# A chunked delta-rule recurrence: two tiles' triangular inverses by 128-wide levels, one tile after the other, or together from 64x64 blocks

## The reference, cut to what matters

```
mod = silu(c) @ ada_w + ada_b              # (1024) @ (1024 x 6144): six rows of 1024
h = rms_norm(x) * (1 + sc1) + sh1          # rows 0, 1: needed first
x = x + g1 * (concat[y_fox, y_rwkv] @ w_out)   # rows 2 to 5: needed after the recurrence
...
def step(S, inp):                          # per head, S is 64x64
    Sa = S @ a_t
    S = S * w_t + Sa (x) b_t + v_t (x) k_t
    return S, S @ r_t
```

## Time and profile before

| | |
|---|---|
| median of 3 runs | 1511.95 us |
| profiled execution, its own time | 1506.93 us |
| its span, first to last instruction | 1505.1 us |
| mean granted TensorE clock | 0.974 |
| PE busy | 1420.7 us, 94% of the span, 7774 MATMUL records |
| DVE busy | 686.7 us, 46% |
| ACT busy | 396.9 us, 26% |
| POOL busy | 121.8 us, 8% |

### The profile page before, as it was taken

The page is one execution under the profiler, slowest core; times in us unless marked ns, Lnnn a source line. Parts: engine busy times, 40 slices in busy tenths (PEclk is TensorE's granted clock), DMA queues, the critical chain, the costliest instruction groups (busy, mean ns, idle before and its releaser), DMA issues.

```text
span 1505.1 us, 19811 instructions
## 1 busy us (share of the span) xinstructions
PE 1420.7 (94%) x7774; PEld 948.3 (63%) x7774; DVE 686.7 (46%) x1234; ACT 396.9 (26%) x636; POOL 121.8 (8%) x67
## 2 busy tenths in 40 slices
PE   5999998899899999999999999999999998999997
PEld 2545698887455444444444444587778657699985
DVE  2054567455761222222222222475356834577763
ACT  0221433300002222222222222245231211354443
POOL 0013346600000000000000000300000000000000
PEclk9999999999989999999999999989979999999999
DMA  9682124411735999999999998555250322155552
GB/s 338 224 270 84 57 82 157 155 57 57 313 144 202 412 418 412 417 413 422 414 413 419 415 412 360 184 210 168 92 104 1 113 75 94 60 193 188 177 195 84
DMA packets 94258, 338.80 MB, mean 225 GB/s; under 512 B 9738, under 2 KB 34842, under 8 KB 65398
## 3 DMA queue, kind: packets, MB, share of 16 engines
q1 hardware_dynamic: 84178, 319.08, 55.1%
q10 hardware_dynamic: 7845, 12.03, 3.1%
q0 software_dynamic: 2176, 6.86, 1.3%
HBM read 332.94 MB, written 1.05 MB: 222 GB/s over the span
## 4 chain that ended last, share of the span: by engine, by line
PE 82%; DVE 12%; DMA 3%; issue 1%; ACT 1%; ACTq 0%; DVEq 0%
PE bank L1751 15%; PE bank L1325 10%; PE bank L1767 8%; PE bank L1340 6%; PE bank L1341 6%; PE bank L1342 6%; PE bank L1311 4%; PE bank L1714 3%; PE bank L1715 2%; PE bank L1732 2%; PE bank L1734 2%; DMA small<-in_norm_g 2%; PE bank L1563 2%; PE bank L1352 2%; PE bank L1567 1%
## 5 line engine op out<-in xcount | busy, mean ns | idle before, releaser
L1325 PE MATMUL bank<-ring,xT 128*128 128x512 f32 (+2 forms) x448 | 182.5, 562 | 8.1 <-DVE xT L2232 5.2
L1325 PEld LDWEIGHTS bank<-ring,xT 128*128 128x128 f32 x448 | 83.4, 195 | 96.0 <-issue 82.8
L1311 PE MATMUL bank<-c_ident 128*128 128x128 f32 (+1 forms) x986 | 132.6, 290 | 0.0
L1311 PEld LDWEIGHTS bank<-c_ident 128*128 128x128 f32 x986 | 126.7, 206 | 5.1 <-issue 4.2
L1767 PE MATMUL bank<-dn,tmp 128*64 128x512 f32 x528 | 120.6, 598 | 0.0
L2763 DVE TENSOR_TENSOR xT<-bank,mod 128x512 fp32r<-128x512 f32 x66 | 45.6, 691 | 158.0 <-ACT mod L1074 150.7
L2756 DVE SCALAR_TENSOR_TENSOR tmp<-silu_c,rc,bank 128x256 f32<-128x256 f32 x33 | 22.6, 684 | 196.8 <-ACT silu_c L1061 191.4
L1340 PE MATMUL bank<-mod,w_high 128*128 128x256 f32 x352 | 98.6, 280 | 1.7 <-DVE xT L3246 1.7
L1341 PE MATMUL bank<-xT,w_high 128*128 128x256 f32 x352 | 98.6, 280 | 0.0
L1342 PE MATMUL bank<-mod,ring 128*128 128x256 f32 x352 | 98.2, 279 | 0.0
L3233 DVE TENSOR_TENSOR ring<-ring,w_high 128x1024 fp32r<-128x1024 f32 x66 | 77.7, 1220 | 21.8 <-ACT w_high L1260 20.1
(11 more groups left out here) (634 smaller groups left out, 2536.0 us busy)
## 6 DMA issues: line engine op xcount, KB each, us to landing
dn<-in_exp_w_down SPq DMA_DIRECT2D x66, 1024.0 KB, 10.4
ring<-in_exp_w_gate SPq DMA_DIRECT2D x34, 1024.0 KB, 10.1
ring<-in_exp_w_up SPq DMA_DIRECT2D x34, 1024.0 KB, 12.1
gu_odd<-in_exp_w_gate SPq DMA_DIRECT2D x32, 1024.0 KB, 9.9
gu_odd<-in_exp_w_up SPq DMA_DIRECT2D x32, 1024.0 KB, 12.0
ring<-in_w_ffn_in SPq DMA_DIRECT2D x22, 1024.0 KB, 5.0
ring<-in_ada_w SPq DMA_DIRECT2D x16, 1024.0 KB, 4.9
ring<-in_w_in SPq DMA_DIRECT2D x7, 2048.0 KB, 11.9
```

The lines of the kernel that those rows point to most:

```text
L1311: pe.matmul(bank[b][:, lo:lo + width], cst["ident"][:, :], cst["ident"][:, 0:width], start=True, stop=True, skip_group_check=True)
L1325: mm = pe.matmul(bank[lin_bank(o)][:, 0:n], lhs(k, t), ring[:, j % RING, k * n:(k + 1) * n], start=(k == 0), stop=(k == kt - 1 and not bias))
```

## The change

Both tiles go through the inverse together. The folded arrays `invs[t]` and `amat[t]` hold, for 8 heads, the two 64x64 diagonal blocks of the 128x128 matrix on top of each other: rows 0 to 63 for the first, 64 to 127 for the second, 8 x 64 = 512 columns. Every product of levels 1 to 5 becomes two products of 64x64 operands (r = 0, 1), one in the upper left and one in the lower right quarter of the array, written to partitions 0 to 63 and 64 to 127 of one bank. All eight heads of a tile fit one bank, so a level has two groups: the two tiles. Level 6 is replaced by a merge: two 64x64 products per head, with a ScalarE copy after each, give the block below the diagonal (`last`), and the solve works with the parts. The products for gram 1 to 3 (`value_grams`) are issued between the levels' products; the first matrices are only made for the diagonal blocks.

The late units are done as `ada_unit` does them: four products of a 32-column weight tile per unit on TensorE, 16 units, ten of them among heads 4 to 7 in place of `keep_warm` products, six behind the heads. There are four slots. The ScalarE scaling, the GpSimd sums and GpSimd's `memset` go. The bias comes in by a load on ScalarE's queue and a VectorE add (`late_sums`). The eight row products stand behind the last read-out instead of in tile 1's levels. The gates of the fox heads move on VectorE from level 2 and 3 of tile 0 to behind the state.

```diff
+    folded += [lv[level][0:BS, 0:BS][np.arange(P) % BS] for level in range(LAST + 1)]
...
-        gram = sb("gram", [P, HEADS, 4, P], wkv_stack)
-        amat = sb("amat", [P, HEADS, P], wkv_stack)
-        inv = sb("inv", [P, HEADS, P], wkv_stack)
-        invT = tmp[:, :].rearrange("p (h c) -> p h c", h=HEADS)
+        gram = (sb("gram", [P, HEADS, 4, P], wkv_stack), gram_1)
+        invs = [sb(f"invs{t}", [P, 2, HEADS, BS], wkv_stack) for t in range(T)]
+        amat = [logw[:, t, :].rearrange("p (h c) -> p h c", c=BS) for t in range(T)]
+        last = [tmp[:, t * W1:(t + 1) * W1].rearrange("p (h c) -> p h c", c=BS) for t in range(T)]
...
+                if u < LATE_SLOTS:
+                    sp.wait_ge(lin_mm, last_of(J_VR if u < LATE_SLOTS // 2 else J_G))
+                else:
+                    sp.wait_ge(late_used, u - LATE_SLOTS + 1)
+                sp.dma_start(late_slot[u % LATE_SLOTS],
+                             A["ada_w"][k * P:(k + 1) * P, (batch + 1) * 2 * D:(batch + 2) * 2 * D])\
+                    .then_inc(ada_full[1 + u % LATE_SLOTS], 16)
...
-            stream(J_OUT, J_OUT + 1)
-            sp.wait_ge(lin_mm, after(("row", N_ROWS - 1)))
-            stream(J_OUT + 1, J_OUT + 2)
+            stream(J_OUT, J_OUT + 2)
...
+            for t in range(T):
+                act.wait_ge(wkv_mm, wkv_count(t, LAST + 1))
+                act.activation(amat[t][BS:P, :, :], heads8(bank[6 + t][BS:P, :]), ACT.Copy).then_inc(wkv_w, 1)
+            for t in range(T):
+                act.wait_ge(wkv_mm, wkv_count(t, LAST + 1, 1))
+                act.activation(last[t][0:BS, :, :], heads8(bank[4 + t][0:BS, :]), ACT.Copy).then_inc(wkv_upd, 1)
...
+            def late_units(n):
+
+                for u in range(late_n[0], late_n[0] + n):
+                    batch, k = u // KT, u % KT
+                    if k == 0:
+                        pe.wait_ge(cb_ready, 2)
+                        pe.wait_ge(lin_evac, after(J_G, batch))
+                    pe.wait_ge(ada_full[1 + u % LATE_SLOTS], 16 * (u // LATE_SLOTS + 2))
+                    for g in range(4):
+                        mm = pe.matmul(bank[batch][32 * g:32 * (g + 1), :], late_cols[:, k, :],
+                                       late_slot[u % LATE_SLOTS][:, g * BANK:(g + 1) * BANK],
+                                       start=(k == 0), stop=(k == KT - 1))
+                    mm.then_inc(late_used, 1)
+                late_n[0] += n
...
-                keep_warm((0, 0, 0, 0, 32, 14, 4, 4)[h], 2, W1 - HD, HD)
+                if h >= 4:
+                    late_units(2)
+                    keep_warm((12, 6, 0, 0)[h - 4], 2, W1 - HD, HD)
...
-                    keep_warm(16 if h == 6 else 0, 2, W1 - HD, HD)
+                    if h == 6:
+                        late_units(2)
...
+            def first_matrices(t):
+
+                banks = (score_bank(), score_bank())
+                for pair in range(4):
+                    for r in range(2):
+                        for g in range(2):
+                            src = tilT_of(t, pair)
+                            mm = pe.matmul(banks[g][halves[r], block_of(pair)], src[halves[g], AT_, halves[r]],
+                                           src[halves[g], BT_, halves[r]], start=True, stop=True)
...
+            def value_grams(n):
+
+                t, pair = n // 4, n % 4
+                pe.wait_ge(gram_evac, 2 * n)
+                src = tilT_of(t, pair)
+                for i, (w, v) in enumerate(((BT_, RT_), (KTT_, AT_), (KTT_, RT_))):
+                    for g in range(2):
+                        mm = pe.matmul(bank[g][:, i * P:(i + 1) * P], src[halves[g], w, :], src[halves[g], v, :],
...
+            def masked_source(t, level):
+
+                pe.wait_ge(wkv_upd, T * (level - 1) + t + 1)
                 for h in range(HEADS):
+                    for r in range(2):
+                        mm = pe.matmul(bank[6 + t][halves[r], block_of(h)], gram[t][halves[r], h, 0, halves[r]],
+                                       invs[t][halves[r], INV, h, :], start=True, stop=True)
...
+            def updates(t, level):
+
+                pe.wait_ge(wkv_w, T * level + t + 1)
+                for h in range(HEADS):
+                    for r in range(2):
+                        mm = pe.matmul(bank[4 + t][halves[r], block_of(h)], amat[t][halves[r], h, :],
+                                       invs[t][halves[r], INV_T, h, :], start=True, stop=True)
+                for h in range(HEADS):
+                    for r in range(2 if level < LAST else 1):
+                        mm = pe.matmul(bank[2 + t][halves[r], block_of(h)], invs[t][halves[r], INV_T, h, :],
+                                       amat[t][halves[r], h, :], start=True, stop=True)
+                mm.then_inc(wkv_mm, 1)
...
+            late_units(2)
+            til_transposes(0)
+            late_units(1)
+            pe.wait_ge(tp_evac, TP_TIL + 4)
+            first_matrices(0)
+            til_transposes(1)
+            transposed_grams(0)
+            pe.wait_ge(fox_out, 1)
+            first_transposes(0)
+            late_units(2)
+            pe.wait_ge(tp_evac, TP_TIL + 8)
+            first_matrices(1)
+            transposed_grams(1)
+            first_transposes(1)
+            late_units(1)
+            pe.wait_ge(sc_evac, SC_GRAM + 4 * T)
+            pe.wait_ge(late_summed, 2)
+            for level in range(1, LAST + 1):
+                for t in range(T):
+                    masked_source(t, level)
+                for t in range(T):
+                    if level < LAST:
+                        value_grams(T * (level - 1) + t)
+                    elif t == 0:
+                        pe.wait_ge(lerp_done, 4)
+                        pe.wait_ge(gram_evac, 2 * 4 * T)
+                        value_products(0, bank[0], 2, True).then_inc(u_mm, 1)
+                    updates(t, level)
+            value_products(1, bank[1], 2, False)
+            for t in range(T):
+                pe.wait_ge(wkv_upd, T * LAST + t + 1)
                 for h in range(HEADS):
+                    mm = pe.matmul(bank[6 + t][halves[1], block_of(h)], gram[t][halves[0], h, 0, halves[1]],
+                                   invs[t][halves[0], INV, h, :], start=True, stop=True)
+                mm.then_inc(wkv_mm, 1)
+            value_products(0, bank[2], 3, False)
+            for t in range(T):
+                pe.wait_ge(wkv_w, T * (LAST + 1) + t + 1)
                 for h in range(HEADS):
+                    mm = pe.matmul(bank[4 + t][halves[0], block_of(h)], amat[t][halves[1], h, :],
+                                   last[t][halves[1], h, :], start=True, stop=True)
+                mm.then_inc(wkv_mm, 1)
+            value_products(1, bank[3], 3, False)
+            pe.wait_ge(u_evac, 1)
+            solved(0, bank[7])
+            keep_warm(4, 4)
+            pe.wait_ge(u_evac, 2)
+            b = score_bank()
+            for pair in range(4):
+                c = slice(pair * P, (pair + 1) * P)
+                pe.matmul(b[:, c], til(BT_, 0)[:, c], rhs_u[:, 1, c], start=True, stop=False)
+                mm = pe.matmul(b[:, c], til(KTT_, 0)[:, c], z_rw[:, 0, 1024 + pair * P:1024 + (pair + 1) * P],
+                               start=False, stop=True)
+            mm.then_inc(sc_mm, 1)
+            read_out(0, bank[2])
+            pe.wait_ge(state_ready, 1)
+            with_state(bank[1], AT_).then_inc(u_mm, 1)
+            with_state(bank[3], RT_)
+            keep_warm(4, 4)
+            pe.wait_ge(u_evac, 4)
+            solved(1, bank[0])
+            keep_warm(4, 4)
+            pe.wait_ge(u_evac, 5)
+            read_out(1, bank[3])
+            for i in range(N_ROWS):
+                o, r = outputs[(("row", i), 0)], slice(i % 4 * 32, i % 4 * 32 + 1)
+                pe.wait_ge(lin_evac, o - 1)
+                pe.matmul(bank[lin_bank(o)][:, :], ones_pp[r, :], late_rows[i // 4][r, :], start=True, stop=True)\
+                    .then_inc(lin_mm, 1)
...
-                pool.tensor_tensor(sums, sums, late_slot[u % 2], ALU.add).then_inc(late_used, 1)
...
+            dve.wait_ge(lin_mm, last_of(J_G))
+            dve.tensor_copy(late_cols, small[:, KT:2 * KT].unsqueeze(2).broadcast_to([P, KT, 32])).then_inc(cb_ready, 1)
...
+                    dve.tensor_tensor(invs[t][:, INV_T, :, :], invs[t][:, INV_T, :, :], a, ALU.add)
+                    link(dve.tensor_tensor(invs[t][:, INV, :, :], invs[t][:, INV, :, :], b, ALU.add))
+                else:
+                    low, high = slice(0, BS), slice(BS, P)
+                    dve.tensor_tensor(invs[t][low, INV, :, :], invs[t][low, INV, :, :], b[low], ALU.add)
+                    dve.tensor_tensor(last[t][high, :, :], invs[t][high, INV_T, :, :], a[high], ALU.add)
+                    link(dve.tensor_tensor(invs[t][low, INV_T, :, :], invs[t][low, INV_T, :, :], a[low], ALU.add))
...
+            til_copies(0)
+            head_outputs()
```

(35 more changed lines are left out.)

354 lines of the change are left out of this document (145 added, 209 removed).

## The result

| | before | after |
|---|---|---|
| median of 5 runs | 1511.95 us | 1455.22 us (1452.51 to 1465.5) |
| profiled execution, its own time | 1506.93 us | 1465.5 us |
| its span | 1505.1 us | 1463.2 us |
| mean granted clock | 0.974 | 0.960 |
| PE busy | 1420.7 us | 1376.7 us, 8116 records |

The ratio is 0.9639 (95% interval 0.9607 to 0.967): faster, by 56.7 us between the medians. The profiled execution lay 10 us above its median, so I read stages from it and totals from medians.

The account below looks back on a forecast made before the run. TensorE was taken as the bound, its levels limited by chained products and masks. The changed part was to end at 307.0 instead of 368.5 us, saving 61.5: 1506.9 - 61.5 + 5.0 = 1451 us, range 1438 to 1486.

Parts of the forecast that it names:

- both tiles' inverses in one stretch, halves overlapping: Levels of both tiles: 64x64 row halves overlap, 0.0325 us per record; 61.5 us saved in all; chance 0.50.
- the slow rival: Levels 1 to 5: small products cost 0.11 us per record, 0.0785 more for 1056 records; 1538 us; chance 0.12.
- The 64x64 record: Small products of the levels: alternating halves cost 0.0325 us per record; ends 0.0275 and 0.055, for safety 0.11.
- starts of the two halves within 0.02 us: Sign that the forecast is right: in the levels, the two row halves' products start nearly together.
- The same-bank rival: Levels: halves writing one bank take turns, 0.0225 us more per small record; 1479 us; chance 0.25.
- Steps 1 and 2: Heads 4 to 7 and tile 0's til copies: 4.5 us new wait, partly half clock; til copies done at 216.2.
- Step 3: From til copies to level 1, both tiles: TensorE and VectorE alternate, 18.0 us; level 1 starts at 234.2.
- Step 4: Levels 1 to 4, both tiles: 8.3 us per level, 33.3 in all, to 267.5.
- step 7: Sixteen 1 MB late-unit loads cost nothing with four slots; J_OUT's weights, asked for by 230, have 70 us.
- Step 5: Level 5, merge and solves to the last read-out: 32.6 us, to 300.1, including 2.4 from the root's order.
- Step 6: Row products behind the last read-out: 16 records x 0.43 = 6.9 us, to 307.0; they save nothing.
- the rival: Six later unit pairs: late units wait for their loads, 2.5 us each time, 15 us; 1466 us; chance 0.10.

Follow-up runs that it names:

- the second profile: Profile of the changed kernel run once more without an edit: 1460.62 us, ratio 0.9664.
- the halves apart: Against the changed kernel, all eight heads of the upper row half before all eight of the lower: 1474.63 us, ratio 0.9743.
- the last kernel: Changed kernel with column copy earlier, root later, keep-warm products among row products, late units moved, J_OUT's loads held back: 1446.08 us, ratio 0.9576.
- the root late: Against the changed kernel, ScalarE's root for the fox heads behind the merge's copies instead of ahead of the first: 1451.82 us, ratio 0.9611.
- the copy first: Against the changed kernel, VectorE's replicated column copy between the two log decays instead of behind both: 1453.29 us, ratio 0.9607.
- the units moved: Changed kernel with the earlier column copy, plus late units of heads 6 and 7 put ahead of decay_sums(1) and behind the heads: 1459.01 us, ratio 0.9648.
- bunching the units: Against the changed kernel, all sixteen late units behind the heads, keep-warm products back in heads 4 to 7: 1476.9 us, ratio 0.9778.

## Why the prediction was right, and where its terms were off

The forecast was 1451, the range 1438 to 1486, the likeliest case "both tiles' inverses in one stretch, halves overlapping". The time was 1455.22, and 1460.62 when run again. The mechanism and the side are right; several terms were too small, and that the total came within 4 us of the first median is luck. Up to J_OUT's second half the sum has 61.5 us saved, the two profiles 46.5 and 47.4 (219.25 less 172.8 or 171.8): 14 to 15 us less. Behind that stretch, where the sum had no change, the second profile is 3.1 us shorter than the trace of before and the first 2.0 longer. The rest of the 56.7 us between the first medians is the spread of single executions, 13 us for this kernel, and no trace places it. (Two slips of the sum itself are small: 1506.9 - 61.5 + 5.0 is 1450.4, and the slow rival's 0.0785 should be 0.0775.) The steps below add up to the 15.0 us by which the first profile misses: 4.7 to the til copy, 3.1 back to level 1, 0.6 in the levels, 7.7 from level 5 to the last read-out, 2.9 in the rows, 2.2 behind them.

- **The 64x64 record, right.** 0.0325 was taken, 0.031 measured, 0.055 to 0.059 with the halves apart. A level of both tiles has a period of 8.36 us (8.3 predicted) where one tile's cost 7.05. Not all of the gain hangs on it: apart, the halves give back 15 us of it, and the kernel stays 36.5 us faster than before. How the other 36 us divide between the two tiles in one stretch, the merge in place of level 6 and the new way of the late units, no run shows. I had named starts of the two halves within 0.02 us as a sign; they are read in no line here, and the spacing stands for them.
- **The same-bank rival, wrong.** The Trainium skill, TensorEngine Tiling (Array Packing), Restrictions and Gotchas, has it that row tiles can't access one PSUM bank at the same time. By that rule a record would have been 0.055; here the halves write different partitions of one bank and 0.031 was measured, so the rule as it stands does not hold for such tiles.
- **Steps 1 and 2, heads: both of its ends happened.** The copy was ready where the sum put it (an idle time of 3.53 us instead of 4.5). I set the til copy at 46; it was at 44.2 where the clock held and at 50.1 to 50.7 where it fell, each a little beyond the end that I had given for it. I had let the clock be low for two units and 24 records only; at 183 to 195 it was low for 12 us.
- **Step 3, stage to level 1, 2.8 too long.** 18.0 from the til copies' end to level 1 was predicted, 15.2 measured (223.2 to 238.4). My handovers of 0.2 us may have been counted where the other queue still had work; that is not shown.
- **Step 4, levels, right** (33.9 and 33.0 from level 1's first product to level 5's, for 33.3). The 0.9 us between the two profiles are level 2's issue wait, 1.62 and 0.72 us. J_OUT's loads, which step 7 had at nothing, run at about 400 GB/s beside it, and with them held back the last kernel has no such wait; but the same loads come with 0.64 us as well as with 1.91, so they cost tenths as a rule.
- **Step 5, level 5 to the last read-out, 7.7 too short** (40.3 for 32.6, 272.3 to 312.6 us; 40.7 in the second profile). I had seen the root ahead of the copies and priced the order at 2.4. Its wait was 1.5; the clock behind it, which the sum did not have, cost the other 6 of the 7.7 us that moving it gives back. With the root late the step takes 33.0, and the sum without its 2.4 has 30.2: 2.8 more is short elsewhere in the chain. This is the largest failed term.
- **Step 6, rows, 2.9 too short, and 2.2 more behind them,** of which J_OUT's first half is 1.5 (15.54 for 14.00). "16 records x 0.43" was the full-clock price without overlap. Four records take 1.13 us at full clock, less than that, but the other twelve ran at half clock, behind a first wait of 0.68 us for ScalarE's copies.
- **Step 7, the late units' loads.** No wait for them in the changed kernel's heads, as predicted; the rival shows as soon as VectorE's wait is removed (0.46 us with the copy first, 1.41 with the units moved), and 7.5 us of such waits are in the 12.3 that bunching the units costs.

What is left open is why the clock falls in the rows or J_OUT's first half in every kernel here. It isn't the single contracted partition, and filling the waits keeps the rows at full clock but not what follows.

## What to carry to other kernels

Split a small product into diagonal quarters and issue the quarters alternately: the order alone takes the spacing from 0.055 to 0.031 us per record here, and was worth 15 us. When a change puts a new wait of 1.5 to 4 us into a stretch where TensorE is the bound, price it as the wait alone and as the wait plus the half clock behind it (some 6 us in either place of this kernel), for both ends of the range, and look first for a copy or a root that can change places in the queue it stands in. Work moved into idle time on one engine brings its loads along: count when each one can start. And when a kernel's medians wander by 5 us between repeats, read an edit from the stage that it touches, in several profiles if you have them.

## What was not expected of the hardware

- Records of 64x64 products that alternate between opposite quarters and write one bank are spaced 0.031 us; one half after another 0.055.
- In the changed kernel's first profile waits of 3.53 and 1.50 us were each followed by 12 to 15 us at a clock of 0.50 to 0.58, with TensorE busy for nearly all of them. The same wait for the copy ahead of the same work did not bring it in two other executions (44.2 against 50.1 us to the til copy); behind the wait for the root it came in all seven.
- At the same place of level 2, beside loads of some 400 GB/s, TensorE's "issue" wait was 0.64 to 0.82 us in six profiles and 1.62 and 1.91 in two; with the loads held back, in one profile, it was gone. That the loads cause it is likely and not shown.
